# A two-layer attention trunk in float32: coefficients of the last group's first pair made within the step, another slot for a gate piece, mixing split three to one

## The reference

```python
# layer 0: banded attention, window 128, a sink logit per head in the denominator
o, _ = banded_attention(q, k, v, SWA_WINDOW - 1, sinks)
return o.reshape(B, S, MIX_WIDTH) * jax.nn.silu(gate)
# layer 1: three (window, dilation) patterns, merged by their denominators
for gi, (window, dil) in enumerate(((128, 1), (512, 4), (2048, 16))):
    ...
    o, lse = dilated_attention(q, k, v, window, dil)
w = jax.nn.softmax(jnp.stack(lses, axis=0), axis=0)
o = jnp.sum(w[..., None] * jnp.stack(outs, axis=0), axis=0)
return o.reshape(B, S, MIX_WIDTH) * jax.nn.silu(gate)
```

## Time and profile before

| | us |
|---|---|
| median of 3 runs | 1393.14 |
| lowest, highest | 1387.77, 1397.15 |
| profiled execution | 1391.8 |
| its span | 1390.0 |
| last step of layer 0, output rows behind it | 318 to 371, 374.6 to 406.5 |
| last step of layer 1, output rows behind it | 1228 to 1273, 1276.3 to 1316.4 |

### The profile page before, as it was taken

One profiled execution on the slowest core, in us unless ns is written; L12 is line 12 of the kernel. 1 busy time (PEld: TensorE's weight loads), 2 busy tenths in 40 slices (PEclk: granted clock), 3 DMA queues, 4 the chain that ended last, 5 costly groups with the idle time before them and its releaser, 6 DMA issues.

```text
span 1390.0 us, 24909 instructions
## 1 busy us (share of the span) xinstructions
PE 1311.0 (94%) x8938; PEld 1222.2 (88%) x8938; DVE 732.3 (53%) x2225; ACT 635.2 (46%) x1767; POOL 397.3 (29%) x443
## 2 busy tenths in 40 slices
PE   4899999999899988999999999999999999998896
PEld 4899998987799888999989999899999899976896
DVE  5544452545652525555436764455654367656625
ACT  6344463545722425454446554346544465544111
POOL 2212051240511111221123833207621238223310
PEclk9999999999999998999999999999999999998998
DMA  5011022121454301011032311212310212133623
GB/s 193 20 31 47 24 62 69 32 76 56 159 163 148 96 27 43 12 40 27 17 84 56 87 54 33 61 35 82 91 29 16 84 56 70 55 94 92 167 91 121
DMA packets 101080, 97.32 MB, mean 70 GB/s; under 512 B 30688, under 2 KB 87520, under 8 KB 100960
## 3 DMA queue, kind: packets, MB, share of 16 engines
q1 hardware_dynamic: 100960, 95.73, 23.2%
HBM read 79.46 MB, written 16.25 MB: 69 GB/s over the span
## 4 chain that ended last, share of the span: by engine, by line
PE 86%; DVE 4%; DMA 3%; ACT 3%; POOL 2%; issue 1%; SPq 1%; DVEq 0%; POOLq 0%; ACTq 0%
PE j_bank L1095 59%; PE s_bank L1196 8%; PE o_bank L1229 7%; PE t_bank L1208 6%; PE j_bank L1175 3%; PE s_bank L1095 1%; DMA w_raw<-in_w_qkv 1%; DMA w_raw<-in_w_out 1%; PE o_bank L1095 1%; DMA gate<-in_positions 1%; DVE ht_lo L1564 1%; POOL xr L1027 1%; ACT probs L1313 1%; DVE qs L1581 1%; DVE w_lo L1495 1%
## 5 line engine op out<-in xcount | busy, mean ns | idle before, releaser
L1095 PE MATMUL j_bank<-w_hi,ht_hi 128*128 128x384 f32 (+1 forms) x1328 | 453.2, 341 | 28.4 <-DVE ht_lo L1686 12.4
L1095 PE MATMUL j_bank<-w_lo,ht_hi 128*128 128x384 f32 (+1 forms) x1328 | 441.0, 332 | 0.0
L1095 PE MATMUL j_bank<-w_hi,ht_lo 128*128 128x384 f32 (+1 forms) x1328 | 440.5, 332 | 0.0
L969 POOL TENSOR_TENSOR w_lo<-w_raw,w_hi 128x768 fp32r<-128x768 f32 (+1 forms) x60 | 102.2, 1703 | 661.4 <-ACT w_hi L1304 660.0
L1095 PEld LDWEIGHTS j_bank<-w_hi,ht_hi 128*128 128x128 f32 x1328 | 253.6, 191 | 41.3 <-issue 29.0
L1095 PEld LDWEIGHTS j_bank<-w_lo,ht_hi 128*128 128x128 f32 x1328 | 254.0, 191 | 0.0
L1095 PEld LDWEIGHTS j_bank<-w_hi,ht_lo 128*128 128x128 f32 x1328 | 253.6, 191 | 0.0
L1313 ACT ACTIVATE probs<-probs,stat 128x256 f32<-128x256 f32 (+1 forms) x512 | 230.6, 453 | 24.4 <-DVE stat L1527 22.5
L1522 DVE CUSTOM_DVE_ANT_0 probs<-s_bank,masks 128x128 f32<-128x128 f32 (+1 forms) x448 | 142.3, 355 | 137.7 <-PE t_bank L1208 133.6
L722 ACT COPY probs_t<-t_bank 128x256 f32<-128x256 f32 (+1 forms) x128 | 57.9, 453 | 320.1 <-PE o_bank L1229 314.9
L1196 PE MATMUL s_bank<-ks,qs 128*128 128x256 f32 (+1 forms) x1024 | 142.2, 281 | 10.3 <-DVE qs L1581 5.6
(11 more groups left out here) (159 smaller groups left out, 1646.1 us busy)
## 6 DMA issues: line engine op xcount, KB each, us to landing
w_raw<-in_w_qkv SPq DMA_DIRECT2D x64, 384.0 KB, 3.4
coef<-coef_dram SPq DMA_DIRECT2D x96, 128.0 KB, 3.0
w_raw<-in_w_gate SPq DMA_DIRECT2D x32, 256.0 KB, 3.3
mix_dram<-xr SPq DMA_DIRECT2D x12, 512.0 KB, 3.5
w_raw<-in_w_out SPq DMA_DIRECT2D x16, 384.0 KB, 3.5
qk<-mix_dram SPq DMA_DIRECT2D x12, 512.0 KB, 4.6
xr<-in_x SPq DMA_DIRECT2D x8, 512.0 KB, 7.2
out<-xr SPq DMA_DIRECT2D x8, 512.0 KB, 2.7
```

What stands on the lines that cost most here:

```text
L969: pool.tensor_tensor(quarter(n, q, 1), raw_quarter(n, q), quarter(n, q, 0).bitcast(F32), ALU.subtract).then_inc(w_lo_done["p"], 1)
L1095: last = pe.matmul(to, a(x_, kt), b(y_, kt), start=(start and kt == kts[0] and x_ == y_), stop=(stop and kt == kts[-1] and x_ == 1))
```

## The change

- The second gate piece of a layer's last step stands in slot 2 instead of 4.
- The last group's first pair: `coefs_first`, `den_exp`, `coefs_last`, the transpose and the copy all stand in the pair of slots 8 and 9 (before: slots 8, 9, 10, 13, 13), and the store and loads in slot 10 instead of 13. The copy goes to a tile of its own, `v`.
- Quarters 2 and 3 of the first output job's weights are split behind the third mixed tile instead of in slot 14. SyncE's loads stay where they were in its queue.
- Behind the last exponentials, mixed tile 0 comes ahead of the copies of the last probabilities; VectorE's copy of the second pair's coefficients comes behind tile 1 instead of 2.
- GpSimd mixes one half (first pair, first half), VectorE the three others, the first of them behind tile 2.
- The next output job's splits stand earlier: ScalarE's and VectorE's for its first quarters around the last two mixed tiles, VectorE's of the later ones ahead of the last copy of a job.

```diff
-            _slots.append((JOBS[-1], [0, 4, 8, 12] if _s.last else [12, 13, 14, 15]))
+            _slots.append((JOBS[-1], [0, 2, 8, 12] if _s.last else [12, 13, 14, 15]))
...
-            _at += [(3, _now[0] + 1, (0,)), (5, _now[0] + 1, (1,)), (14, _now[0] + 1, (2, 3))]
+            _at += [(3, _now[0] + 1, (0,)), (5, _now[0] + 1, (1,))]
+            END_SPLIT[_layer] = [(_now[0] + 1, 2), (_now[0] + 1, 3)]
...
-END_FIRST, END_EXP, END_LAST, END_TURN, END_COPY = 8, 9, 10, 13, 13
+END_TURN, END_STORE = 9, 10
+
+END_HALVES = {"p": [(0, 0)], "v": [(0, 1), (1, 0), (1, 1)]}
...
# SyncE
-                            raws_after(SPLIT_BEHIND.get(s.t, []))
+                            raws_after(SPLIT_BEHIND.get(s.t, []) if not s.last else END_SPLIT[layer])
...
-                            if slot == END_COPY:
+                            if slot == END_STORE:
                                 coef_store(s, 0)
                                 end_coefs(s, 0)
...
# GpSimd
-                end_mix(steps[-1], 0)
+                end_mix(steps[-1])
+                w_lo(END_SPLIT[layer])
...
# ScalarE
+                        if END_TURN in pair and s.last:
+                            den_exp(s, 0)
...
                 last = steps[-1]
-                for u in range(UNITS - TURN_BACK, UNITS):
-                    empty_turn(last, u)
...
                     if k == 0:
+                        empty_turn(last, UNITS - 2)
                         den_exp(last, 1)
                     if k == 1:
                         silu(last)
+                    if k == 2:
+                        w_hi(END_SPLIT[layer])
+                w_hi(splits_of("mid-job", layer, 0))
...
# VectorE
+                        if END_TURN in pair and s.last:
+                            coefs_first(s, 0)
                         b, u = unit_before(s, a + 1, TURN_BACK)
                         if b:
                             empty_turn(b, u)
+                        if END_TURN in pair and s.last:
+                            coefs_last(s, 0)
...
                 coefs_first(last, 1)
                 mix_split(layer, 0, mix_in[0])
+                empty_turn(last, UNITS - 1)
                 store_ot(last, 1, 1)
                 coefs_last(last, 1)
                 for k in range(1, MIX_LOADS):
                     mix_split(layer, k, mix_in[k % 3])
+                    if k == 1:
+                        coef_copy(last, 1)
                     if k == 2:
-                        coef_copy(last, 1)
+                        end_mix(last, 0)
+                        w_lo(END_SPLIT[layer])
                 mix_split(layer, MIX_LOADS, ot[out_region(last)][:, 0, :])
                 end_mix(last, 1)
+                end_mix(last, 2)
                 mix_split(layer, MIX_LOADS + 1, ot[out_region(last)][:, 1, :])
                 for c in range(OUT_PARTS):
-                    w_lo(splits_of("job", layer, c))
+                    if c == 0:
+                        w_lo(splits_of("mid-job", layer, c))
                     for k in range(NB):
+                        if k == NB - 1 and c + 1 < OUT_PARTS:
+                            w_lo(splits_of("job", layer, c + 1))
                         empty_piece(("out", layer, c, k))
-                        if k == 2:
+                        if k == 2 and c > 0:
                             w_lo(splits_of("mid-job", layer, c))
```

More of the change, by code:

```diff
@@ L474, in coef_rows_of @@
             rows = comb_rows(s, coef_calls(s)[k])
-            if s.last and k == 1:
-                return v[0:rows.stop - rows.start, 1 - s.t % 2, 0:2, :].rearrange("p a b -> p (a b)")
+            if s.last:
+                return v[0:rows.stop - rows.start, 1 - s.t % 2, 2 * k:2 * k + 2, :].rearrange("p a b -> p (a b)")
             return coef_rows[0:rows.stop - rows.start, :]
@@ L605, in mix_links_before, with half_links, end_count, wait_end_mixed @@
             return sum(mix_links(s) for s in STEPS[:t] if s.ends_group and not s.last)
-        def end_links(layer):
-            return sum(mix_links(LAYER_STEPS[n][-1], (0,)) for n in range(layer + 1))
+        def half_links(layer):
+            return 2 if layer == 0 else 6
+        def end_count(by, layer, halves):
+            return len(END_HALVES[by]) * sum(half_links(n) for n in range(layer)) + halves * half_links(layer)
+        def wait_end_mixed(eng, layer, pair):
+            for by in "pv":
+                eng.wait_ge(end_mixed[by], end_count(by, layer, sum(r <= pair for r, _ in END_HALVES[by])))
         def coef_loads_before(t):
@@ L794, in end_coefs @@
                 sp.wait_ge(scored, UNITS * s.t + NB * (r + 1))
+                if s.layer == 1 and r == 0:
+                    sp.wait_ge(mixed, mix_links_before(s.t))
                 for p in range(1 if s.layer == 0 else 3):
@@ L835, in res_load @@
                 elif c == 1:
[L837 to L838 removed]
+                    wait_end_mixed(sp, layer, 1)
                 else:
@@ L1015, in mix @@
                     link(pool.tensor_tensor(into, into, opened, ALU.mult), done + 1)
[L1017 to L1022, removed]
-                    into = half_blocks(ot[out_region(s)][:, r, :], s.layer, half)
[L1024 to L1027, removed]
-                    if p > 0:
-                        done += 1
-                        end_link(pool.tensor_tensor(into, into, tile, ALU.add), done)
-                    if p == (0 if s.layer == 0 else 2):
-                        done += 1
-                        opened = half_blocks(gate_of(s.layer, s.g)[:, r, :], s.layer, half)
-                        pool.wait_ge(silued, groups_before(s.t) + 1)
-                        end_link(pool.tensor_tensor(into, into, opened, ALU.mult), done)
@@ new lines, in end_mix @@
+            def end_mix(s):
+                for n, (r, half) in enumerate(END_HALVES["p"]):
+                    done = end_count("p", s.layer, n)
+                    pool.wait_ge(ot_stored, 4 * s.t + 2 * r + 2)
+                    into = half_blocks(ot[out_region(s)][:, r, :], s.layer, half)
+                    for p in range(1 if s.layer == 0 else 3):
+                        tile = half_blocks(ot[(out_region(s) + p) % 4][:, r, :], s.layer, half)
+                        by = coef_end[r][p].rearrange("p (f n i) -> p f n i", f=2, n=4)[:, half, :, :]
+                        pool.wait_ge(end_in[3 * r + p], 32 * (1 + (s.layer == 1 and p == 0)))
+                        done += 1
+                        end_link(pool.tensor_tensor(tile, tile, by, ALU.mult), done)
+                        if p > 0:
+                            done += 1
+                            end_link(pool.tensor_tensor(into, into, tile, ALU.add), done)
+                    pool.wait_ge(silued, groups_before(s.t) + 1)
+                    opened = half_blocks(gate_of(s.layer, s.g)[:, r, :], s.layer, half)
+                    end_link(pool.tensor_tensor(into, into, opened, ALU.mult), done + 1)
@@ L1469, in _ @@
                     w_hi(splits_of("job", layer, c))
-                    w_hi(splits_of("mid-job", layer, c))
+                    if c > 0:
+                        w_hi(splits_of("mid-job", layer, c))
                 if layer == 0:
```

49 lines of the change are left out of this document (21 added, 28 removed).

## The result

The changed kernel takes 1407.34 us (median of 4 runs, 1402.45 to 1408.30), the kernel before 1390.99 us in the same comparison (4 runs, 1387.77 to 1397.15): ratio 1.0105, 95% interval 1.006 to 1.015. Run again it gave 1405.70 us (6 runs), ratio 1.0098, interval 1.0081 to 1.0116. So it is 1% slower, and 1407 lies above the top of the forecast range (1403), 12 us above the forecast of 1395.

The account below looks back on a forecast made before the run. TensorE, busy 94% of the span, was taken as the bound, its waits and low clock alone open to change. Terms -1.0 - 2.7 - 1.1 - 3.3 + 9.9 + 10.2 - 8.1 - 0.8 gave +3.1 us on 1391.8: 1395, range 1385 to 1403.

Parts of the forecast that it names:

- step 4: SyncE's queue: tile 3's load waits behind the moved weight split, delaying row 3; +9.9 us layer 0, +10.2 layer 1.
- step 6: Output jobs: splits one copy earlier shorten TensorE's wait at a job's start; 0.4 us each, -0.8 us.
- step 5: Mixing one half GpSimd, three VectorE: layer 1's wait before its last row goes, with its low clock; -8.1 us.
- rival (b): Layer 1's last-pair coefficients land too late for VectorE's last two halves; last-row wait stays, 1403 us; chance 0.12.
- Step 1: Last steps, gate piece to slot 2: both 2.80 us waits go (-4.5, -6.3 with clock), partly offset by later waits.
- steps 1 and 2: Each layer's last step, gate piece and first pair's coefficients moved: together -1.0 us in layer 0, -2.7 in layer 1.
- Step 3: Weight split leaves slot 14, so the first output job's row 0 starts earlier: -1.1 us layer 0, -3.3 layer 1.
- Steps 2 and 6: First pair's coefficients in pair 8: 0.8 us wait in layer 0, 0 in layer 1; earlier output-job splits: -0.8 us.
- (a): Tile 3 is not late, but most of the last-row wait's 8.1 us comes back: 1383 us; chance 0.13.
- (c): Last steps' two pairs without a piece wait 2.8 us each and drop the clock as before: +4.3, 1399; chance 0.13.
- (d): VectorE's blocking on the transpose is shorter, last steps and row 0 starts save their upper bounds: -7, 1388; chance 0.12.

Follow-up runs that it names:

- the first experiment on the queue: Changed kernel with SyncE's two raw weight loads moved behind its asks for mixed tiles 3 to 5: 1389.61 us, ratio 0.9985.
- The best kernel: Changed kernel with SyncE's two weight loads behind tiles 3 to 5 and last-pair coefficients, ScalarE's next-job split behind the last two tiles: 1379.30 us, ratio 0.9908.

## Why the prediction failed

The forecast was no measurable change, +3.1 us; it is +10.7 in the changed stretches and about 1% by the medians. Of the 12 us between 1395 and 1407, the changed stretches make 7.6. The forecast was counted from a profiled execution that spent less outside the changed stretches than any other (1141.8 us), which can make up for the rest. The chain that it named as the cost is the cost: putting SyncE's two loads elsewhere took the loss away. Term by term, forecast and measured (means of two profiles each):

| | forecast | measured |
|---|---|---|
| step of layer 0, with row 0's start | -2.1 | -2.2 |
| rows of layer 0 (step 4) | +9.9 | +9.7 |
| step of layer 1, with row 0's start | -6.0 | -2.7 |
| rows of layer 1 (steps 4 and 5) | +2.1 | +6.7 |
| output jobs (step 6) | -0.8 | -0.8 |
| sum | +3.1 | +10.7 |

**The step that failed is step 5**, "TensorE, held up by step 4, wants it at 32.3", ready at 31.0, so no wait. TensorE wanted it at 32.5 after row 0's end (1292.5), as forecast; it was ready at 35.8. This is rival (b), to which I gave 0.12 and a deciding point of 21.3 for the landing: VectorE's three waits for coefficients ended at 21.9, 24.3 and 26.8 (counted from 1292.5). They make 3.45 of the 4.8 us; most of the rest is tile 6, done at 21.2 instead of 20. What I had not counted is the store. I put the loads at "12 to 16"; they were asked for from 16.8 on, since the store that they wait for took 7.3 us behind three tiles issued at once, not the 3.1 that it took behind one. Without those 4.2 us all three waits would be gone, and the tile ready when TensorE wants it (an estimate from these rows). The mechanism of step 4 bunches the tiles, and so makes its neighbour late as well: the two costs were one event, and I treated them as independent. The wait of 5.04 went down only to 3.28, and the 7.2 us behind it ran at 0.76.

**Step 4** came out right in sum by luck, as errors cancel in layer 0. VectorE's split ended 6.5 us after row 0's end instead of 4.8 (the mixing product of 2.29 us, where I had put 0.72); the tile landed 6.2 us after it was asked for instead of 4.9. That 4.9 was not measured with two quarters just ahead, as I had read it: in the kernel before they were asked for at 369.70 and 371.42 and had landed by 374.14, before the tile was asked for. Nor is it the two tiles behind that make it late: in the run with the split alone three tiles went out together too, with only one quarter just ahead, and the first of them landed in 3.8 and 3.6 us. So the wait was 10.33, not 7.1. Against that, the clock behind it cost 6.5 x 0.23 = 1.5 us, not 2.8, and I forgot a gain: with no wait ahead of row 0 its low clock goes as well, 6.4 us to 3.8. In layer 1 the split ended at 7.1 (forecast 7.0), the tile landed 5.8 us after its asking, the wait was 8.79 (forecast 7.5).

**Step 1, layer 1**, was mis-sized, and with it the whole 3.3 us of that step's row in the table. From the fills to the end of the last exponentials layer 1's step took 42.3 and 40.7 us before, 41.7 and 42.3 after: 0.5 more, where steps 1 and 2 forecast 2.7 less. The two waits of 2.80 went, but others came (1.44 us in both profiles, 0.96 in the first, and late in the step 2.13 in the second where 1.17 had stood), and the clock did not come back. I had put down 1.8 us less of low clock; TensorE's busy time in the step was 39.5 and 38.1 us before and 39.0 and 40.0 after, for the same matmuls. In both profiles of the changed kernel the window of some 30 us around the end of that step reads 0.84; before, the 31.3 us ahead of row 0 read 0.92. The experiment that puts the gate piece back in slot 4 says the same: nothing gained in layer 1. In layer 0 steps 1 and 2 gave 0.9 us (46.9 to 46.5 and 45.6), with 1.0 forecast.

**Step 3** holds: from the end of the exponentials to row 0's start it was 6.6 us in both layers and is 5.3 in layer 0 and 3.5 and 3.3 in layer 1, so 1.3 and 3.2 less where 1.1 and 3.3 were forecast. One reading in it was wrong: the small operation of 1.45 us (1271.72 to 1273.17) had GpSimd's split of weights beside it (1271.29 to 1273.14), not its mixing. That split has left the place too, so the step came out.

**Steps 2 and 6** hold: TensorE waits 1.12 us for layer 0's coefficients (forecast 0.8), and the output jobs are 0.8 us shorter in every kernel with that edit.

**The rivals.** (a), tile 3 not late, was made by hand in the first experiment on the queue; it said 1383 and that the last row's wait would come back, and it did, by 8.19 us, for 1389.6. (c) and (d) were about terms of one to three us and can't be told apart by medians that spread over 10. By the rows (c) is wrong in layer 0 (a wait of 1.48 us, not 2.8, and a clock of 1.00 behind it) and right in layer 1 about the clock alone.

What stays open: why the clock falls behind the same short waits in one execution and not in another; why the first tile lands so much later behind two quarters than behind one; and 2 to 6 us by which the medians differ more than the changed stretches do.

## What to carry to other kernels

When work is moved later on one engine, list every in-order queue in which something waits for it, and what stands behind that wait; then do the same again once the first is mended. Here each edit was harmless or good only with its neighbours: the moved split needs its loads behind the tiles, those need ScalarE's split behind the last tiles, and all three together, with the rest of the change, beat the kernel before by 0.9% where the first alone is 1.5% slower. And price a small store on which others wait by what is queued ahead of it, not by its size. That it would pay to put it ahead of the bulk loads follows from these rows, but no run here did it.

## What the runs showed of the hardware

A store of 24 KB landed 7.3 us after its issue behind three tiles (1.5 MB) issued just ahead in the same queue, 3.1 us behind one tile and 2.8 us behind two weight quarters; in layer 0 one of 8 KB took 7.5 us behind three tiles. In each of these places it landed 0.17 us after the last load ahead of it (in the kernel before at 1288.92, the tile at 1288.75). (The Trainium skill, DMA: Bandwidth & Descriptors, "Two DMAs through the same engine are not ordered", says that within one queue of a DMA engine descriptors start in order; that agrees.)

The spread of one kernel's runs goes with TensorE's mean clock. Of 35 runs of the kernel before, those at 0.972 took 1396.3 to 1397.9 us and those at 0.981 or 0.982 took 1387.7 and 1388.9. The best kernel's five runs spread over 3.4 us only, at 0.982 and 0.983.
